# A hybrid decoder step on one core: weight splits, the v rows and the last combine move between engines

## The reference

```python
proj = rms_norm(x, norm_g) @ w_in
u, v, xr, g_a, g_b = jnp.split(proj, SPLITS, axis=-1)
v = layer_norm(jax.nn.gelu(v), ln_g, ln_b)
y_a = chunk_spatial_gating(jax.nn.gelu(u), v, w_s, b_s)
xc, new_buf = causal_depthwise_conv(xr, conv_buf, conv_w, conv_b)
y_b, h_last = rg_lru(xc, h0, lam, w_a, b_a, w_x, b_x)
merged = jax.nn.sigmoid(g_a) * y_a + jax.nn.sigmoid(g_b) * y_b
x1 = x + merged @ w_out        # v of the last chunk is an output too
y = x1 + hier_moe(rms_norm(x1, norm2))   # 2 of 32 experts per row
out = rms_norm(y, norm_f)
```

## Time and profile before

| | |
|---|---|
| median of 3 runs | 665.38 us (664.79 to 667.03) |
| the profiled execution | 664.86 us, span 663.2 us |
| mean granted clock of TensorE | 0.966 |
| busy: TensorE, VectorE, ScalarE, GpSimd | 574.3, 317.0, 226.5, 71.5 us |
| DMA | 160.60 MB, mean 242 GB/s |

### The profile page before, as it was taken

The page is one execution under the profiler, slowest core; times in us unless marked ns, Lnnn a source line. Parts: engine busy times, 40 slices in busy tenths (PEclk is TensorE's granted clock), DMA queues, the critical chain, the costliest instruction groups (busy, mean ns, idle before and its releaser), DMA issues.

```text
span 663.2 us, 8776 instructions
## 1 busy us (share of the span) xinstructions
PE 574.3 (87%) x2808; PEld 351.3 (53%) x2808; DVE 317.0 (48%) x653; ACT 226.5 (34%) x390; POOL 71.5 (11%) x136
## 2 busy tenths in 40 slices
PE   3899899999999999999899888999998879977700
PEld 3676596877778777777478533433333333322200
DVE  5834667767768677677557863100100000100038
ACT  5423425465573755747163211111111111111122
POOL 1100070000000000004000011212112111210000
PEclk9899999999999999999899979999999899999965
DMA  8421324832222222221593679999999999999764
GB/s 311 150 76 65 127 80 173 343 104 71 75 64 93 100 71 95 84 82 63 188 408 119 246 308 421 419 419 419 420 420 421 420 420 421 420 419 421 302 265 167
DMA packets 33447, 160.60 MB, mean 242 GB/s; under 512 B 6320, under 2 KB 6704, under 8 KB 21008
## 3 DMA queue, kind: packets, MB, share of 16 engines
q1 hardware_dynamic: 27808, 149.52, 57.1%
q0 software_dynamic: 5472, 10.63, 4.4%
q10 hardware_dynamic: 144, 0.15, 0.1%
HBM read 155.01 MB, written 14.17 MB: 255 GB/s over the span
## 4 chain that ended last, share of the span: by engine, by line
PE 58%; SPq 18%; DVE 11%; DMA 7%; ACT 3%; issue 2%; DVEq 0%; ACTq 0%; POOLq 0%; POOL 0%
SPq L530 15%; PE ps L1417 13%; PE ps L1419 12%; PE ps L1418 12%; PE ps L1764 6%; DMA wslot<-in_wmoe 4%; PE ps L1788 4%; PE ps L1535 2%; PE ps L1567 2%; DVE x L1398 2%; DMA raw<-in_wmix 1%; PE ps L1621 1%; PE ps L1519 1%; SPq L563 1%; PE ps L1558 1%
## 5 line engine op out<-in xcount | busy, mean ns | idle before, releaser
L1764 PE MATMUL ps<-wslot,xgT 128*64 128x512 f32 x528 | 123.8, 601 | 16.2 <-DMA wslot<-in_wmoe 14.7
L697 ACT ACTIVATE wh<-raw 128x1024 fp32r<-128x1024 f32 x56 | 59.1, 1057 | 163.6 <-PE ps L1419 143.9
L1417 PE MATMUL ps<-xh,wh 128*128 128x512 f32 x256 | 102.5, 400 | 0.0
L1419 PE MATMUL ps<-xl,wh 128*128 128x512 f32 x256 | 99.9, 390 | 0.0
L1418 PE MATMUL ps<-xh,wl 128*128 128x512 f32 x256 | 99.8, 390 | 0.0
L1764 PEld LDWEIGHTS ps<-wslot,xgT 128*64 128x64 f32 x528 | 41.0, 138 | 94.9 <-issue 93.1
L897 DVE TENSOR_TENSOR wl<-raw,wh 128x1024 fp32r<-128x1024 f32 x53 | 66.6, 1256 | 48.7 <-ACT wh L697 47.7
L1788 PE MATMUL ps<-wslot,hT 128*64 128x512 f32 x264 | 62.1, 598 | 8.3 <-ACT hT L862 7.6
L1363 DVE SCALAR_TENSOR_TENSOR hm<-ps,rt,hs 128x256 f32<-128x256 f32 x12 | 5.8, 483 | 125.9 <-ACT hs L860 125.9
L1417 PEld LDWEIGHTS ps<-xh,wh 128*128 128x128 f32 x256 | 48.1, 188 | 16.1 <-issue 6.7
L1419 PEld LDWEIGHTS ps<-xl,wh 128*128 128x128 f32 x256 | 48.0, 188 | 10.6
(11 more groups left out here) (299 smaller groups left out, 773.6 us busy)
## 6 DMA issues: line engine op xcount, KB each, us to landing
wslot<-in_wmoe SPq DMA_DIRECT2D x97, 1024.0 KB, 27.5
raw<-in_wmix SPq DMA_DIRECT2D x56, 512.0 KB, 4.2
gy<-ytok SPq DMA_DIRECT2D x8, 512.0 KB, 6.6
xt<-in_x SPq DMA_DIRECT2D x4, 512.0 KB, 6.8
x<-in_x SPq DMA_DIRECT2D x4, 512.0 KB, 4.5
xnd<-x SPq DMA_DIRECT2D x4, 512.0 KB, 5.5
wslot<-in_wmoe SPq DMA_DIRECT2D x4, 512.0 KB, 27.0
out_y<-yf SPq DMA_DIRECT2D x4, 512.0 KB, 2.6
```

The source lines that it names most:

```text
L697: a.activation(WH[hslot], raw[:, slot, :, :].rearrange("p k c -> p (k c)"), ACT.Copy).then_inc(hi_ready, 1)
L1417: pe.matmul(out, sh, mh_, start=start, stop=False)
L1419: return pe.matmul(out, sh, ml_, start=False, stop=stop)
L1764: l = pe.matmul(ps[CAP * s:CAP * s + CAP, 2, :], xgT[:, c, CAP * s:CAP * s + CAP], wslot[q][s][:, c * 512:(c + 1) * 512], start=c == 0, st ...
```

## The change

1. VectorE makes all low parts. Those of units 42, 43 and 44 (`EARLY`) are placed in the last channel: before the scan, behind the state rows, and behind `merged`. The rotation of the three slots for split weights changes with it (`split_at`), and ScalarE no longer waits for unit 40 before the high part of unit 42.
2. VectorE makes `vo`; GpSimd only stores it. GpSimd's memset of `xg` is gone.
3. At the end of v, ScalarE copies `sp` before the high part of unit 9.
4. TensorE runs four extra products on `ident` at the start (`keep_warm`).
5. The last two scatters take their offsets from `idx` without a copy.
6. The read-back is sent half by SyncE and half by ScalarE, in the order tile 0, sample rows, tiles 1, 2, 3. ScalarE loads the table of the root ahead of it.
7. The sample rows are combined by TensorE: x1 times the identity, plus each read-back times a diagonal matrix of gates (`dgs`), in PSUM. Lengths are taken in the order 0, 1, sample, 2, 3.
8. Mean and EPS are the scale and bias of ScalarE's root.

```diff
@@ -48,11 +48,13 @@
 ORDER_A = ((0, 0), (0, 1), (0, 2), (1, 0), (0, 3), (1, 1), (1, 2), (1, 3))
-POOLED = range(O_FIRST + 2, O_FIRST + 5)
+EARLY = range(O_FIRST + 2, O_FIRST + 5)
 TILE_AT = (0, 1, 4, 2, 3)
...
 OUTC = 36
+LENGTHS = (0, 1, NT, 2, 3)
+READ = (0, NT, 1, 2, 3)
 (C_G1, C_W0, C_CB, C_LAM, C_BA, C_BX, C_H0, C_ST, C_G2, C_LG, C_LB) = (0, 1, 5, 6, 7, 8, 9, 17, 41, 42, 43)
...
@@ -398,14 +401,7 @@
-            return (n - O_FIRST) % 2 if n < O_FIRST + 3 else (2, 1, 0)[(n - O_FIRST) % 3]
...
-        def lo_done(e, n):
...
-            if n in POOLED:
-                e.wait_ge(lo_pool, n - POOLED[0] + 1)
-            else:
-                e.wait_ge(lo_ready, n + 1 if n < POOLED[0] else n + 1 - len(POOLED))
+            return (n - O_FIRST) % 3
@@ -476,7 +472,7 @@
-                lo_done(e, n - 4)
+                e.wait_ge(lo_ready, n - 3)
                 if n < O_FIRST + UNITS_O + RAW:
@@ -568,12 +564,11 @@
             e.sem_inc(held, 1)
-            for t in range(TILES):
+            for t in READ:
                 r = rowsof(t)
-                for s in range(2):
-                    e.dma_start(gy[0:r, s, t, :], ytok[s * TA + t * P:s * TA + t * P + r, :]).then_inc(back_in[t], 16)
-            for t in range(TILES):
-                e.wait_ge(fin_ready, t + 1)
+                e.dma_start(gy[0:r, 0, t, :], ytok[t * P:t * P + r, :]).then_inc(back_in[t], 16)
+            for n, t in enumerate(LENGTHS):
+                e.wait_ge(fin_ready, n + 1)
                 e.dma_start(y_tiles[t], yf[0:rowsof(t), t, :]).then_inc(done_out, 16)
@@ -609,13 +604,6 @@
-            g.wait_ge(v_ready, 1 + TILES)
-            g.wait_ge(const_in, NCONST - 16)
-            g.tensor_tensor(vo[:, 0, :], v[:, NT - 1, :], lng[:], ALU.mult).then_inc(vo_ready, 1)
-            g.tensor_tensor(vo[0:S, 1, :], v[0:S, NT, :], lng[0:S, :], ALU.mult).then_inc(vo_ready, 1)
-            g.wait_ge(vo_ready, 2)
-            g.tensor_tensor(vo[:, 0, :], vo[:, 0, :], lnb[:], ALU.add).then_inc(vo_ready, 1)
-            g.tensor_tensor(vo[0:S, 1, :], vo[0:S, 1, :], lnb[0:S, :], ALU.add).then_inc(vo_ready, 1)
             g.wait_ge(vo_ready, 4)
@@ -624,13 +612,7 @@
-            for n in POOLED:
-                h = split_at(n)
-                g.wait_ge(hi_ready, n + 1)
-                g.tensor_tensor(WL[h], raw[:, n % RAW, :, :].rearrange("p k c -> p (k c)"), WH[h].bitcast(F32),
-                                ALU.subtract).then_inc(lo_pool, 1)
             g.wait_ge(unit_done, STEPS)
-            g.memset(xg[:], 0.0).then_inc(xg_zero, 1)
@@ -645,6 +627,12 @@
                 gather_at(colg[:, 0:1])
...
+            def scatter_at(offsets):
...
+                g.indirect_dma_start(
+                    out=ytok, out_offset=bass.IndirectOffsetOnAxis(ap=offsets, axis=0),
+                    in_=yo[:, :], in_offset=None, bounds_check=2 * TA - 1, oob_is_err=False).then_inc(y_out, 16)
...
@@ -680,7 +665,9 @@
             for n in (2, 1):
-                scatter(idxx, bass.ds(nx + (TAIL - n), 1), nx + (PAIRS - n + 1))
+                g.wait_ge(yo_sb, FIRST + nx + (PAIRS - n + 1))
+                g.sem_inc(held, 1)
+                scatter_at(idx[:, 1, PAIRS - n:PAIRS - n + 1])
@@ -728,12 +715,15 @@
                     a.wait_ge(unit_done, n + 1)
+                    if n == UNITS_V - 1:
+                        a.activation(sp[:], ps[:, sbank, :], ACT.Copy).then_inc(vsum, 1)
                     split_hi(n + 2, (n + 2) % RAW, n % 2, 16 * ((n + 2) // RAW + 1))
...
                         a.activation(v[0:S, NT, 0:512], ps[0:S, v_banks(0)[2], :], ACT.Gelu_apprx_tanh).then_inc(v_gelu, 1)
-                a.activation(sp[:], ps[:, sbank, :], ACT.Copy).then_inc(vsum, 1)
+                if half == 0:
+                    a.activation(sp[:], ps[:, sbank, :], ACT.Copy).then_inc(vsum, 1)
                 for t in range(NT):
@@ -813,7 +803,7 @@
                 n = O_FIRST + m
-                a.wait_ge(unit_done, max(n, O_FIRST + 1))
+                a.wait_ge(unit_done, n)
                 if m in (5, 8):
@@ -874,15 +864,26 @@
                 expert_pass(m + HEAD, rtx[:, bass.ds(m, 1)], True)
+            a.activation(warm[:], ones[:, 0:1], ACT.Sqrt)
             a.dma_start(st, so[:]).then_inc(done_out, 16)
...
-            for t in range(TILES):
+            a.wait_ge(y_out, nx * 16 + 16 * PAIRS)
+            a.sem_inc(held, 1)
+            for t in READ:
                 r = rowsof(t)
-                a.wait_ge(comb, 2 * t + 2)
-                a.wait_ge(n2_sq, 2 * TILES + t)
-                a.activation(junk3[0:r, :], x1[0:r, t, :], ACT.Square, accum_out=ss[0:r, t:t + 1]).then_inc(n2_sq, 1)
-                a.wait_ge(fin_ms, t + 1)
-                a.activation(rstd[0:r, t:t + 1], ss[0:r, t:t + 1], ACT.Sqrt).then_inc(fin_sq, 1)
+                a.dma_start(gy[0:r, 1, t, :], ytok[TA + t * P:TA + t * P + r, :]).then_inc(back_in[t], 16)
...
+            for n, t in enumerate(LENGTHS):
+                r = rowsof(t)
+                if t == NT:
+                    a.wait_ge(sample_mm, 1)
+                    rows_ = ps[0:S, 4:6, :].rearrange("p b c -> p (b c)")
+                else:
+                    a.wait_ge(comb, 2 * t + 2)
+                    rows_ = x1[:, t, :]
+                a.wait_ge(n2_sq, 2 * TILES + n)
+                a.activation(junk3[0:r, :], rows_, ACT.Square, accum_out=ss[0:r, t:t + 1]).then_inc(n2_sq, 1)
+                a.wait_ge(n2_sq, 2 * TILES + n + 1)
+                a.activation(rstd[0:r, t:t + 1], ss[0:r, t:t + 1], ACT.Sqrt, scale=1.0 / D, bias=eps[0:r, :]).then_inc(fin_sq, 1)
...
@@ -1010,6 +1012,12 @@
             split_lo(0, 2, UNITS_V + 3)
+            d.wait_ge(v_ready, 1 + TILES)
+            d.tensor_tensor(vo[:, 0, :], v[:, NT - 1, :], lng[:], ALU.mult).then_inc(vo_ready, 1)
+            d.tensor_tensor(vo[0:S, 1, :], v[0:S, NT, :], lng[0:S, :], ALU.mult).then_inc(vo_ready, 1)
+            d.wait_ge(vo_ready, 2)
+            d.tensor_tensor(vo[:, 0, :], vo[:, 0, :], lnb[:], ALU.add).then_inc(vo_ready, 1)
+            d.tensor_tensor(vo[0:S, 1, :], vo[0:S, 1, :], lnb[0:S, :], ALU.add).then_inc(vo_ready, 1)
@@ -1027,6 +1035,10 @@
             smp = lambda t: t[:, SEQ:TA].rearrange("p (b s) -> p b s", b=DB)
+            def early_lo(n):
...
+                split_lo(split_at(n), n % RAW, n + 1)
...
             def channel(j, last):
@@ -1072,9 +1084,13 @@
                 own.then(d.memset(smp(A)[:, :, 0], 0.0))
+                if last:
+                    early_lo(EARLY[0])
                 own.then(d.tensor_tensor_scan(XC[:], A[:], TI[:], 0.0, ALU.mult, ALU.add))
...
                 own.then(d.tensor_copy(sj[:, 1:9], smp(XC)[:, :, DS - 1]))
+                if last:
+                    early_lo(EARLY[1])
@@ -1088,7 +1104,9 @@
                                 ALU.subtract).then_inc(merged, 1)
-                if not last:
+                if last:
+                    early_lo(EARLY[2])
+                else:
                     split_lo(0, 2, j * 4 + (n0 + 7))
@@ -1225,7 +1243,7 @@
                     add_rows(0, 4, O_BANKS[0][1])
-                if m < 2 * UNITS_O - 2 and n + 2 not in POOLED:
+                if m < 2 * UNITS_O - 2 and n + 2 not in EARLY:
                     split_lo(split_at(n + 2), (n + 2) % RAW, n + 3)
@@ -1295,6 +1313,8 @@
             own.then(d.tensor_tensor(gate[:, 1, :], gate[:, 0, :], r1[:, 3, :], ALU.mult))
+            for s in range(2):
+                d.tensor_scalar(dgs[:, s, :], ident[0:S, 0:S], gate[0:S, s, POS[NT]:POS[NT] + 1], None, ALU.mult).then_inc(dgs_ready, 1)
@@ -1378,40 +1398,44 @@
-            def mean_square(t):
-                r = rowsof(t)
-                d.wait_ge(n2_sq, 2 * TILES + 1 + t)
-                d.tensor_scalar(ss[0:r, t:t + 1], ss[0:r, t:t + 1], 1.0 / D, EPS, ALU.mult, ALU.add).then_inc(fin_ms, 1)
...
-            def final(t):
-                r = rowsof(t)
-                d.wait_ge(fin_sq, t + 1)
-                own.then(d.reciprocal(rstd[0:r, t:t + 1], rstd[0:r, t:t + 1]))
-                d.scalar_tensor_tensor(out=yf[0:r, t, :], in0=x1[0:r, t, :], scalar=rstd[0:r, t:t + 1], in1=nf[0:r, :],
-                                       op0=ALU.mult, op1=ALU.mult).then_inc(fin_ready, 1)
...
-            d.wait_ge(const_in, NCONST)
-            for t in range(TILES):
-                r = rowsof(t)
+            def combine(t):
...
                 d.wait_ge(back_in[t], 32)
                 for s in range(2):
-                    d.scalar_tensor_tensor(out=x1[0:r, t, :], in0=gy[0:r, s, t, :], scalar=gate[0:r, s, POS[t]:POS[t] + 1],
-                                           in1=x1[0:r, t, :], op0=ALU.mult, op1=ALU.add).then_inc(comb, 1)
+                    d.scalar_tensor_tensor(out=x1[:, t, :], in0=gy[:, s, t, :], scalar=gate[:, s, POS[t]:POS[t] + 1],
+                                           in1=x1[:, t, :], op0=ALU.mult, op1=ALU.add).then_inc(comb, 1)
                     if s == 0:
                         d.wait_ge(comb, 2 * t + 1)
```

(36 more changed lines are left out.)

32 lines of the change are left out of this document (14 added, 18 removed).

## The result

The changed kernel takes **661.90 us** (median of 5 runs, 660.23 to 663.20) against 665.38 us (5 runs, 663.93 to 667.03) of the kernel before on the same chip: ratio 0.9945, 95% interval 0.9924 to 0.9967. It is 3.5 us faster. I had predicted 658.4, a gain of 7.0, and a range that ended at 661.4.

What follows compares the result with a forecast made beforehand. TensorE's products bound the first part, the expert-weight stream the next, VectorE the tail; 0 + 1.0 + 0 + 3.8 + 2.2 = 7.0 us won gave 657.9 against the profiled execution, 658.4 against the median; range 655.7 to 661.4.

Steps and rivals of the forecast that it cites:

- The start, 0: Start of the kernel: four extra TensorE products on ident neither win nor lose; bounds 0.2 us gained, 0.65 lost.
- The rival's price of 1.9 us: Rival, kernel start: the early warm-up keeps TensorE at 2.4 GHz, 1.9 us more won, 656.5 us; chance 0.08.
- The end of v, 1.0 won: End of v: ScalarE copies sp before unit 9's high part, so TensorE's fold starts 0.97 us earlier.
- The v rows, 0: VectorE making the v rows: four operations of 1.23 us finish in time for TensorE; 0, bound 0.5 us lost.
- The early splits, 3.8 won: Output projection: low parts of units 42 to 44 on VectorE; 2.4 us at unit 44 plus 1.8 from the clock, bounds 3.56 and 4.2.
- no stretch below 0.9 from 300 to 372 us: Sign of being right: TensorE's granted clock never below 0.9 between 300 and 372 us in the profile after.
- The tail, 2.2 won: After the weight stream, from the last scatter to the last store: 2.2 us won in all, bounds 1.0 and 3.2.
- The read-back up to the first combine: Tail: tile 0's two read-backs go at once on two queues, 0.3 us won.
- VectorE's part: Tail: VectorE's combines and final products take 18.0 us instead of 20.3, 2.3 won, with 0.5 allowed for tile 1 landing later.
- Last store: End of the tail: the last store is a full tile, 2.6 us to landing instead of 1.9, 0.7 lost.
- The stream does not absorb: Rival denied here: expert weights sent earlier only wait for each other, the projection's 3.8 us is lost, 662.2 us; chance 0.06.
- The clock rival: Rival, output projection: the clock stays low behind unit 44's shorter wait, 1.8 us not won, 660.2 us; chance 0.17.

Runs made afterwards that it cites:

- the one-queue run: The changed kernel with all ten read-backs of the tail on SyncE's queue instead of half on ScalarE's; 660.38 us, ratio 0.9920 to the kernel before.
- the logits apart: The 32 small router logits products split in two places, tile 1's moved behind unit 10; on the changed kernel 658.89 us (0.9895), on the kernel before 664.21 us (0.9985).

## Why the prediction was wrong

- **The start, 0**: right in the sum, for a reason I did not give. The clock was up at 24 us in the changed kernel's profile, by the counts not through the warm-up (3 of 14 profiles with it, 2 of 6 without), and VectorE's chain takes the 1.7 us back at 33 us. The rival's price of 1.9 us rested on the wrong wait.
- **The end of v, 1.0 won**: right. The fold waits 0.78 instead of 1.80 us, and at the first units of the projection the lead is 0.9.
- **The v rows, 0**: right. VectorE's split takes 1.21 us, the four operations end at 90.69, zT starts at 90.62, and TensorE shows no wait in its 64 products.
- **The early splits, 3.8 won**: right up to 341 us (5.0 - 1.0 = 4.0; the wait before unit 44 is 1.13 for 1.5), and the cause is shown: GpSimd's subtractions back, the slow operations back. All three of these were the maxima of their lines, not only the last two. What failed is the sentence that whatever ends the projection earlier brings everything behind it forward one for one. It held for the stream, which moved by the full lead in the one-queue run. It did not hold for TensorE's clock. I had weighed the clock at the one place where the trace of before showed it low, behind unit 44, and put 1.8 us of gain there in the sum; I did not ask where else the granted clock could fall once that place was gone. It fell behind the logits and took 3.2 us in the changed kernel's profile, 1.9 on average over the nine profiles, while behind unit 44 it had cost 1.6 (2.9 in the second profile of before). So the 1.8 us of the clock was not won: the loss stood in another place. Of the signs I named, no stretch below 0.9 from 300 to 372 us is the one that the profile broke.
- **The tail, 2.2 won**: mis-sized. Scatter 0.4 for 0.3. The read-back up to the first combine: 0.66 lost for 0.3 won, to which the new order and the second queue both add. VectorE's part: 1.7 for 2.3; tile 1 came 1.19 us late, for 0.5, since I took the sample rows' 0.26 MB at the full 420 GB/s and they pass at about half that. Last store 0.76 lost for 0.7. The sum is 0.7, below my bound of 1.0.
- **The rivals.** The stream does not absorb (656.9 with its lead intact). The clock rival had the right engine and size, but tied the loss to unit 44's wait; and no case had a low clock behind the logits. Its time, 660.2, is nearer to the measured one than the forecast, but by another place. Of the signs of being wrong, no wait of VectorE for the sample rows came in the changed kernel.

For the profiled pair: 7.0 less 3.2 at the logits, 1.5 in the tail and 1.7 at the last pair (a fall that only four of the twenty profiles have), plus 0.8 that the stream regained (lead 1.85 behind the logits, 2.6 at the last weights) is 1.4; the spans differ by 1.6. The medians differ by more, 3.5, probably because the low stretches do not fall alike in all executions. With averages in place of this one profile, 7.0 less 1.8 for the clock's gain that was not won and 1.5 for the tail is 3.7, an estimate from the losses above. With the logits apart the changed kernel is at 658.9, near the 658.4 of the forecast, and by the ratios 6.0 us below the kernel before with the same edit.

**What stays open.** Why the clock falls behind the logits in the kernels with the change and not in the kernel before was not shown. The count is 8 of 9 against 0 of 2, and two profiles of the kernel before are few. With the logits apart the loss is absent in 9 of 9. That a low stretch just before (unit 44) spares the next one fits the counts, except that the one-queue run had neither. The 1.0 us of the kernel before with its logits apart is within its interval, so some of its executions may lose there too. That the low clock at the logits takes time in the changed kernel is shown by the edit that removes it; that this loss makes up the gap to the forecast rests on the averages.

## What to carry to other kernels

A lead on a busy TensorE is worth its time only if the clock behind it holds: look in the trace not only where the granted clock was low, but at each thin stretch (small products, transposes, waits) that the change moves, and try breaking long thin stretches up among dense ones: here the low clock behind the logits was then gone in 9 of 9 profiles, for 3.3 us in the changed kernel and 1.8 on average over six pairs. One profile shows one draw of the clock, so take several before you price a low stretch. Among read-backs a transfer over few rows belongs last: it moves at a fraction of the rate, and of the three places tried only the last left the other tiles nearly alone. And do not give VectorE long work beside an elementwise operation of GpSimd: the three operations that it had held up for 6 us were the part of this change that paid.

## What had not been expected

- The same wait of 3.17 us before unit 44 was followed by half clock in four profiles and by full clock in one.
- A read-back of 32 rows of 4 KB amid others brings the rate from 400 to 238 GB/s with the DMA share at 1.04: the share reads as full while half the rate is lost.
- A 512 KB store cut in halves on two queues ended 1.1 us later than as one transfer on one queue (one profile).
- In two different places of the program, a low stretch of TensorE's clock cost one of the same two sizes, 1.6 or about 3 us.
